# Modulation groups summed on TensorE: 32 stationary columns in four quarters, and the first four groups straight from their weights

## What is computed

```python
c_act = jax.nn.silu(c)                                    # one row of 1024
mod = (c_act @ w_mod[l] + b_mod[l])[:, None, :]           # w_mod is 1024 x 6144
shift_m, scale_m, gate_m, shift_f, scale_f, gate_f = jnp.split(mod, 6, axis=-1)
h = rms_norm(x, norm_mix[l]) * (1.0 + scale_m) + shift_m
z = h @ w_in[l]                                           # 29 tiles of 256 columns
```

## Time and profile before

| | us |
|---|---|
| median of 3 runs | 2066.38 |
| lowest, highest | 2065.59, 2069.41 |
| the profiled execution, whole run | 2065.59 |
| its span, first to last instruction | 2063.5 |

### The profile page before, as it was taken

How to read it: one execution, slowest core, us unless ns; L and a number is a source line. 1 busy time by engine, 2 the same in 40 slices (tenths; PEclk the granted TensorE clock), 3 DMA queues, 4 the chain that set the end, 5 groups by cost and what they waited for, 6 DMA issues and landing times.

```text
span 2063.5 us, 31497 instructions
## 1 busy us (share of the span) xinstructions
PE 2015.8 (98%) x13041; PEld 1797.7 (87%) x13041; DVE 1703.4 (83%) x1874; ACT 1256.3 (61%) x1269; POOL 39.6 (2%) x77
## 2 busy tenths in 40 slices
PE   7999999999999999999999999999999999999997
PEld 6888999999888899999888888888888888888886
DVE  6787787989787668888369899898888989898887
ACT  3468745554444554443457777777777777777775
POOL 3010000000000000000000000000000000000000
PEclk8999999999999999999999999999999999999999
DMA  9974675768644349999359999999999999999994
GB/s 310 293 239 139 209 255 200 256 227 281 216 164 144 123 159 327 325 308 307 121 175 371 367 345 370 349 366 355 356 358 353 365 361 358 358 355 364 365 367 158
DMA packets 337571, 589.07 MB, mean 285 GB/s; under 512 B 10517, under 2 KB 150315, under 8 KB 337424
## 3 DMA queue, kind: packets, MB, share of 16 engines
q1 hardware_dynamic: 333776, 580.70, 80.4%
q0 software_dynamic: 3008, 5.78, 1.0%
q10 hardware_dynamic: 640, 0.52, 0.1%
HBM read 585.89 MB, written 1.07 MB: 284 GB/s over the span
## 4 chain that ended last, share of the span: by engine, by line
PE 89%; DVE 6%; ACT 2%; issue 2%; DMA 1%; SPq 0%; DVEq 0%; ACTq 0%
PE bk L657 15%; PE bk L659 15%; PE bk L658 15%; PE bk L651 11%; PE bk L653 11%; PE bk L652 11%; DVE wlo L1957 1%; PE bk L1202 1%; DVE macc L1982 1%; ACT whi L1339 1%; DMA raw<-in_w_mod 1%; PE bk L729 1%; PE bk L1251 1%; PE bk L713 1%; PE bk L1114 1%
## 5 line engine op out<-in xcount | busy, mean ns | idle before, releaser
L1957 DVE TENSOR_TENSOR wlo<-raw,whi 128x2048 fp32r<-128x2048 f32 x477 | 1080.6, 2268 | 230.7 <-ACT whi L1339 229.9
L1339 ACT CAST whi<-raw 128x2048 fp32r<-128x2048 f32 x477 | 903.0, 1894 | 394.3 <-PE bk L659 259.2
L651 PE MATMUL bk<-HH,whi 128*128 128x256 f32 x1480 | 424.8, 287 | 1.4 <-DVE KC L2231 1.0
L652 PE MATMUL bk<-HL,whi 128*128 128x256 f32 x1480 | 417.1, 282 | 0.0
L653 PE MATMUL bk<-HH,wlo 128*128 128x256 f32 x1480 | 416.9, 282 | 0.0
L657 PE MATMUL bk<-whi,xh 128*128 128x512 f32 x896 | 354.7, 396 | 0.0
L659 PE MATMUL bk<-wlo,xh 128*128 128x512 f32 x896 | 349.5, 390 | 0.0
L658 PE MATMUL bk<-whi,xl 128*128 128x512 f32 x896 | 348.7, 389 | 0.0
L651 PEld LDWEIGHTS bk<-HH,whi 128*128 128x128 f32 x1480 | 282.2, 191 | 7.0 <-issue 3.8
L652 PEld LDWEIGHTS bk<-HL,whi 128*128 128x128 f32 x1480 | 282.3, 191 | 1.1 <-issue 0.7
L653 PEld LDWEIGHTS bk<-HH,wlo 128*128 128x128 f32 x1480 | 282.2, 191 | 0.0
(11 more groups left out here) (378 smaller groups left out, 2486.0 us busy)
## 6 DMA issues: line engine op xcount, KB each, us to landing
raw<-in_moe_w SPq DMA_DIRECT2D x334, 1024.0 KB, 5.7
raw<-in_ada_w SPq DMA_DIRECT2D x56, 1024.0 KB, 5.4
raw<-in_ff_w SPq DMA_DIRECT2D x40, 1024.0 KB, 5.7
raw<-in_w_in SPq DMA_DIRECT2D x29, 1024.0 KB, 5.4
raw<-in_w_mod SPq DMA_DIRECT2D x24, 1024.0 KB, 6.0
raw<-in_w_up SPq DMA_DIRECT2D x22, 1024.0 KB, 5.4
raw<-in_attn_w_qkv SPq DMA_DIRECT2D x12, 1024.0 KB, 5.3
raw<-in_w_branch SPq DMA_DIRECT2D x8, 1024.0 KB, 5.2
```

The lines of the kernel that those rows point to most:

```text
L651: pe.matmul(o, sh, mh, start=start, stop=False, skip_group_check=True)
L652: pe.matmul(o, sh, ml, start=False, stop=False, skip_group_check=True)
L1339: act.copy(whi[k][:, :n], raw[q.slot[i]][:, :n]).then_inc(q.hi_done.mark(g), 1)
L1957: dve.tensor_tensor(wlo[k][:, :n], raw[q.slot[i]][:, :n], whi[k][:, :n].bitcast(F), ALU.subtract).then_inc(q.taken.mark(i), 1)
```

## The change

All four first groups go direct (`pe_mod_direct`), so DVE sums none of them. The function now handles one slab (`k0`) for each call and uses 32 stationary columns for a matmul instead of 128: four matmuls for each 128 columns, which write the four quarters of PSUM's partitions (128 matmuls a group instead of 32). `pe_mods`, for the later groups, also goes from 64 to 32 columns, 16 matmuls a group instead of 8. The stream brings tiles 0 and 1 of z before group 1 and uses slots 3 and 0 for them. Group 2 is summed before the transposes of x, the two slabs of group 3 between its sums of squares, group 0 after them; group 1 stands between the first and the second half (k = 0 to 3, k = 4 to 7) of z's tiles 0 and 1, of which both first halves now run before both second halves. The spare matmuls are gone. ACT's first split moves behind blocks 0 to 3 of HH; DVE's splits of tiles 0 and 1 move behind blocks 0 to 3 of HL.

```diff
         first = [s for g in (2, 3, 0, 1) for s in mslabs(wmod, g, 0)]
-        st_order = first + order[0:3]
+        st_order = first[:6] + order[0:2] + first[6:] + order[2:3]
...
-        early = (6, 7, 8, 0, 1, 2, 3, 6, 8)
+        early = (6, 7, 8, 0, 1, 2, 3, 0, 6, 8)
         for i, entry in enumerate(st_order):
-            st.add(entry, early[i] if i < 9 else (i - 9) % NR)
-
-        for i in (4, 5):
+            st.add(entry, early[i] if i < 10 else (i - 9) % NR)
+
+        for i in (0, 1, 2, 3, 4, 5, 8, 9):
             _, g, k0 = st_order[i][1]
             st.direct[g, k0] = i
@@ pe_mods
-                    for r in (0, 64):
-                        t = pe.matmul(u.t[r:r + 64, j:j + 1], acc[:, j * 128 + r:j * 128 + r + 64], one[:, 0:1],
+                    for r in range(0, 128, 32):
+                        t = pe.matmul(u.t[r:r + 32, j:j + 1], acc[:, j * 128 + r:j * 128 + r + 32], one[:, 0:1],
                                       start=True, stop=True, skip_group_check=True)
@@ pe_mod_direct
-        def pe_mod_direct(ring, g):
+        def pe_mod_direct(ring, g, k0):
+            u = B.at["mod", pmod[0]] if k0 else take(ring, "mod", pmod[0])
+            i = st.direct[g, k0]
+            w = raw[st.slot[i]]
+            pe.wait_ge(st.raw_in[st.slot[i]], 16 * st.use[i])
+            for k in range(4):
+                for j in range(4):
+                    for r in range(0, 128, 32):
+                        c = k * 512 + j * 128 + r
+                        t = pe.matmul(u.t[r:r + 32, j:j + 1], w[:, c:c + 32], csil[:, 4 * k0 + k:4 * k0 + k + 1],
                                       start=(k0 + k + j == 0), stop=(k0 == 1 and k == 3), skip_group_check=True)
+            t.then_inc(st.summed.mark(i), 1)
+            if k0:
+                u.told = st.summed.now()
+                pmod[0] += 1
@@ pe_start
-            yield from pe_mods(Z_T, -1, 1)
+            pe.wait_ge(*(yield from N.of("csil")))
+            for k0 in range(2):
+                pe_mod_direct(Z_T, 2, k0)
...
+            pe_mod_direct(Z_T, 3, 0)
             yield from pe_stats(Z_S, "x0", 4)
+            pe_mod_direct(Z_T, 3, 1)
             yield from pe_stats(Z_S, "x0", 6)
-            yield from pe_mods(Z_T, -1, 2)
-            pe.wait_ge(*N.at["csil",])
-            pe_mod_direct(Z_T, 0)
-            yield from pe_mods(Z_T, -1)
+            for k0 in range(2):
+                pe_mod_direct(Z_T, 0, k0)
@@ pe_mixer
-            for t in range(2):
-                u = take(Z_G, "z", t)
-                if t == 0:
-                    spare(u.t[:, 0:128], 14)
-                h, l, _ = yield from slab(st, ("z", zjob[t][2]))
-                for k in range(8):
...
+            us = [take(Z_G, "z", t) for t in range(2)]
+            parts = []
+            for half in range(2):
+                if half:
+                    for k0 in range(2):
+                        pe_mod_direct(Z_T, 1, k0)
+                for t in range(2):
+                    if half == 0:
+                        parts.append((yield from slab(st, ("z", zjob[t][2]))))
+                    h, l, _ = parts[t]
+                    for k in range(4 * half, 4 * half + 4):
                         pe.wait_ge(*(yield from xlo_done.of("h0", k)))
...
@@ act_start
-            yield from act_hi(st, 0)
             half = act_modulate("h0", HH, 0, 0, sqb)
...
                 if k == 0:
+                    yield from act_hi(st, 0)
                     yield from act_hi(st, 1)
@@ dve_start
-            yield from dve_mslabs(2)
-            yield from dve_mods(-1, 1)
-            yield from dve_mslabs(4)
             yield from dve_mods(-1, 2)
             yield from dve_coeff("h0", 0, "norm_mix", 0, 2)
...
-            yield from dve_mslabs(st.gi[0])
-            yield from dve_lo(st, 0)
             yield from dve_mods(-1, 3)
...
+            yield from dve_lo(st, 0)
+            yield from dve_lo(st, 1)
             yield from dve_mods(-1)
             for c in range(4, 8):
                 yield from low(c)
-            yield from dve_lo(st, 1)
             yield from dve_lo(st, 2)
```

More of the change, by code:

```diff
@@ L732, in pe_mods @@
                 pmod[0] += 1
-        def pe_mod_direct(ring, g):
[L736 to L743, removed]
+        def pe_mod_direct(ring, g, k0):
[8 more added lines that the diff above has]
+                        t = pe.matmul(u.t[r:r + 32, j:j + 1], w[:, c:c + 32], csil[:, 4 * k0 + k:4 * k0 + k + 1],
                                       start=(k0 + k + j == 0), stop=(k0 == 1 and k == 3), skip_group_check=True)
-                t.then_inc(st.summed.mark(i), 1)
-            u.told = st.summed.now()
-            pmod[0] += 1
+            t.then_inc(st.summed.mark(i), 1)
+            if k0:
+                u.told = st.summed.now()
+                pmod[0] += 1
         def pe_stats(ring, name, c, halves=False):
@@ L881, in pe_mixer @@
         def pe_mixer():
-            for t in range(2):
-                u = take(Z_G, "z", t)
-                if t == 0:
-                    spare(u.t[:, 0:128], 14)
-                h, l, _ = yield from slab(st, ("z", zjob[t][2]))
-                for k in range(8):
-                    if t == 0:
-                        pe.wait_ge(*(yield from xlo_done.of("h0", k)))
[L890 to L895, removed]
+            us = [take(Z_G, "z", t) for t in range(2)]
[9 more added lines that the diff above has]
+                    for k in range(4 * half, 4 * half + 4):
+                        pe.wait_ge(*(yield from xlo_done.of("h0", k)))
+                        for m in range(2):
+                            cols = slice(m * 128, (m + 1) * 128)
+                            tt = three(us[t].t[:, m * S:(m + 1) * S], (h[:, k, cols], l[:, k, cols]), (HH[:, k, :], HL[:, k, :]),
+                                       k == 0 and m == 0, k == 7)
+                    if half:
+                        tt.then_inc(st.slab_done.mark(t), 1)
+                        us[t].told = st.slab_done.now()
             yield from pe_z_side(1)
```

## The result

The change makes the kernel slower: the median of five runs is 2074.76 us (2073.44 to 2078.14) against 2066.38 before (2065.59 to 2069.41), a ratio of 1.0038 [1.0025, 1.005]. The forecast was 2059, its range 2055 to 2073. The profiled execution after took 2074.76 us with a span of 2072.7, 9.2 us more than before.

A forecast was written before the change was run, and what follows sets the result against it. PE was taken to bound the kernel (busy 98% of the span, 89% of the chain). Later groups -5.6 and start -1.8 gave -7.4 us, from the 2066.38 median to 2059 us, range 2055 to 2073.

The forecast's parts named there:

- Price of a small matmul: 32-column matmuls on PE: four column blocks abreast, 7 ns a record at 2.4 GHz and 13 at 1.2.
- Later groups: The 36 later modulation groups: 28 on the chain save 0.20 us each, -5.6 us; bounds -6.6 and +13.
- Only pairs abreast: Rival, chance 0.13: only two column blocks overlap, 14.5 ns a record at 2.4 GHz, 27 at 1.2; 2072 us.
- 29 ns a record: Rival, chance 0.06: small matmuls get no cheaper per record, start +13 us and later groups +13; 2092 us.
- Supply of instructions: Rival, chance 0.17: instruction supply limits PE, 36 ns a matmul, slab 2.3 us; start +2.5, later groups -3.7; 2065 us.
- The start: Up to the end of the second z tile: 53.0 against 54.8 us, -1.8 us, bounds -3.4 and 0.
- Group 0's sum: In the start: second slab lands at 27.0, sum ends at 28.7, DVE's addition at 29.0 instead of 40.47 us.
- First halves: Of z tiles 0 and 1: 48 matmuls, some 17 at doubled time, 7.5 us, ending at 42.6.
- group 1 and its handover: Between the z halves: sum 1.9 to 3.4 us, to 45.3, handovers through DVE and ACT 1.15, to 46.5.
- second halves: Of z tiles 0 and 1: 48 matmuls, 5.8 us to 52.3, up to 1.9 more if the clock fell; 53.0 taken.
- Added waits: SP's stream waits for PE's sum of group 3 (about 23 us); transfers don't break off unless it is later than 27.
- the sign of an error: Forecast wrong if PE is full of the direct line from 10 to 35 us, or z's first half starts after 38.

The follow-up runs named there:

- run 6: Kernel before plus 256 unused 32-column matmuls that wait for nothing, at 673 us, where the weight stream pauses: 2080.84 us in one run.
- run 1: Kernel before with only the edit of `pe_mods` (macc groups' matmuls at 32 columns instead of 64), start's order unchanged: 2062.12 us, 0.997 of the kernel before.
- run 3: Changed kernel with 64 instead of 32 stationary columns in the direct sums, 1024 instead of 2048 instructions: 2072.76 us, ratio 1.0025.
- Run 4: Changed kernel with 128 stationary columns in the direct sums, 512 instructions: 2099.37 us in its one run.
- run 7: Changed kernel's stream order, z halves and later groups, but only group 0 direct, at 64 columns, with 11 spare matmuls kept: 2062.18 us, ratio 0.9976.
- run 8: Changed kernel's stream order, z halves and later groups, but only group 0 direct, at 32 columns, with 11 spare matmuls kept: 2068.44 us, ratio 1.0007.
- run 2: Changed kernel with `pe_mods` for the later groups back at 64 columns, start untouched: 2081.08 us, ratio 1.0064.

## Why the prediction was wrong, point by point

- **Price of a small matmul: nearly right.** Four column blocks do go abreast. At the lower clock a record took 2.65 us / 187 = 14 ns (the row at 34.31, granted clock 0.50; forecast 13); at the higher 1.25 / 128 = 9.8 ns in run 6 (forecast 7). "Only pairs abreast" and "29 ns a record" both fall. The Trainium skill ("TensorE: Matmul & The Clock Gate", section "Wait — 56ns, not 53.3ns?") has about 25 ns as the least distance between matmuls; with 32 columns in four column blocks these traces have 9.8 ns in the mean over 128 records, so here the measurement decides.
- **Later groups: right.** Forecast 0.36 us of chain each and -5.6 us in all; measured 0.36, and -5.4 behind the start of the changed kernel, -6.3 by the medians of run 1. The 5.4 is the shift of the second z tile's end less the change of the profiled span. The same subtraction gives a gain of 3.7 us in run 1 and of 4.2 to 4.4 in runs 3, 4, 7 and 8, and 0.15 in run 2, which keeps 64 columns. So these runs put the gain between 3.7 and 6.3 us, no closer, and the forecast lies inside. 64 instructions a group lie in the 256 that a piece brings, and PE is busy with long matmuls before and after, so a piece is there in time; PE's idle time in front of these matmuls is 0.8 us in all, put down to ACT and not to issue (the row of L729 above).
- **Supply of instructions: the step that failed.** The forecast prices a slab by the array alone, 0.93 to 1.7 us, with nothing for the supply, and so has group 0's addition at 29.0; it ran at 43.07. The prediction had the cause as a rival with 0.17, at 36 ns a matmul, or 2.3 us a slab, and so no loss; the 64 matmuls of a piece in 6.4 us are 100 ns each. It took for the bound the pace at which 16 records of one group had run, and those were few enough to lie in one piece. The term is not a rate per matmul but one piece of 256 instructions, in 6.4 to 7.0 us beside the stream: a slab of 256 instructions costs up to 6.4 us or more where nothing else fills the time. A count would have said so: up to the end of group 0 PE has some 1600 instructions (1536 direct, and two for each of 32 records of transposes and square sums), 440 of them had run before the first stall, and the other 1160 are 4.5 pieces. The fifth packet began 23.6 us after the first (39.4 and 15.8, a mean of 5.9 each); its instructions ran at 41.89. The one shorter distance among them, 4.0 us (28.7 to 32.7), lies where the share of the transfer engines was 0.35.
- **The start, by its terms.** Forecast end of the second z tile 53.0, measured 69.39, 16.4 later. Group 0's sum: 28.7 forecast, by the landing of its slab; 43.05 measured, by PE's order. Of these 14.35, 12.14 are the three stalls; 10.44 us of direct work agree with six slabs at 1.7; the transposes and square sums took 9.2 in place of 6.6. From the sum to the first z matmul 6.3 (forecast 6.4). First halves 8.4 in place of 7.5 (by its own parts, 17 matmuls at 0.24 and 31 at 0.12, the forecast should have said 7.8), since the matmuls stay at 0.21 us each up to 54.6; group 1 and its handover 4.2 with a stall of 0.48 (3.9); second halves 7.4 (6.5). These four add 2.0. The stretches (columns as above):

```profile
14.33:18.25 3.92, 0.00 (x1) 0.00 (x0) 0.00 (x0) 0.00 (x0) 3.62 (x7) 1.00 1.07 357
27.99:31.28 3.29, 0.00 (x1) 0.00 (x1) 0.00 (x0) 0.00 (x0) 0.00 (x0) 0.95 0.35 113
36.96:41.89 4.93, 0.00 (x1) 0.00 (x0) 0.96 (x3) 0.00 (x0) 0.00 (x0) 0.50 1.03 383
49.30:57.60 8.30, 8.26 (x48) 8.22 (x48) 1.99 (x1) 0.00 (x0) 0.00 (x0) 0.67 0.81 260
```

  In the three stalls PE, its loads and DVE have next to nothing; the second fits no lack of bandwidth, as the share is 0.35 (SP had stopped, below), yet the piece still took 2.6 us from its packet to its first matmul.
- **Added waits: right in kind.** SP did stand behind group 3's sum, and because that sum ended at 32.31 and not 23, the transfers did break off (0.35 of the share). The weights behind it landed at 38.75, before anything asked for them, so it cost nothing that shows.
- **What was named as the sign of an error** is what happened: z's first half started after 38 (49.34). PE's stretch between 10 and 35 us was full of the direct line and of holes in it.
- **The chances** don't add up as they stand: by their parts "same" is 0.24 (0.07 of the forecast and the supply's 0.17) and "slower" 0.23 (0.13, 0.06 and 0.04), not 0.26 and 0.20.

## What to carry to other kernels

Count instructions as well as array time. On this chip PE had 256 instructions for every 6.4 to 7 us beside a full weight stream (3.5 to 3.7 with the transfer engines idle), so a run of several hundred matmuls that PE could finish faster than that is bound by it (32 columns here), and one that takes longer is not (64 columns at 1.2 GHz, 6.92 us for 256 instructions, ran without a stall in run 3); the packets of the instruction queue divide the program into such pieces, and an "issue" gap in the middle of a row of like instructions is its sign. Where few small matmuls stand between long ones, as in the later groups, cutting the stationary columns and using the four column blocks pays in full.

## What the runs showed of the hardware that was not expected

- A piece of instructions is 16 KB, 256 instructions, and comes later beside data transfers: 6.4 to 7.0 us from piece to piece with the engines at a share of 1.05, 3.5 to 3.7 at 0.02. What sets the 3.5 us that are left was not tried.
- A matmul of f32 with 32 stationary columns and one moving column, in four column blocks in turn, takes 9.8 ns a record at 2.4 GHz and 14 to 14.8 at 1.2: not twice, while with 128 columns it is 112 and 207 ns. What sets the 9.8 was not tried.
- The granted clock doesn't tell the level at the start. In run 3 the same 64 pairs took 6.92 us twice, at 1.00 and at 0.50 in the record (columns as above):

```profile
11.34:18.26 6.92, 6.92 (x130) 6.91 (x130) 0.00 (x0) 0.27 (x1) 6.49 (x13) 1.00 1.06 367
30.48:37.40 6.92, 6.92 (x129) 6.84 (x128) 2.46 (x6) 0.89 (x2) 0.00 (x0) 0.50 1.05 376
```

  A pair at 2.4 GHz takes 58 ns, so PE worked at 1.2 GHz in both. Since 6.92 us for 256 instructions is also about the distance of two pieces, the supply is a rival for this pace. Run 4 rules it out: with 128 columns, 64 records (128 instructions) take 13.6 us at a recorded 1.00, 213 ns each, close to the 207 of the earlier trace rows at 0.50.

```profile
11.21:24.80 13.59, 13.59 (x66) 13.59 (x66) 0.00 (x0) 0.27 (x1) 7.97 (x16) 1.00 1.06 350
```

  So the 1.00 of these first stretches is no measurement of the clock.
